# The plan of the expert passes moved from a stage of its own into the mix, and the experts' credits from GpSimd to TensorE

## The reference, cut to what matters

```python
x  = x + mix @ w_out
x  = x + memory_cross_attention(rms_norm(x, g_mem_norm), rms_norm(mem, g_mem_src), ...)
x  = x + moe_ffn(rms_norm(x, g_moe_norm), ...)
# moe_ffn: 32 experts, 4 per token
logits = t @ router_w + router_b
top_logit, top_idx = top_k(logits, 4);  gates = softmax(top_logit)
gu = t[tok] @ w_gate_up[e] + b_gate_up[e]
act = (clip(gu[:, 1::2], -7, 7) + 1) * gate * sigmoid(1.702 * gate)   # gate = min(gu[:, 0::2], 7)
out[tok] += gates * (act @ w_down[e] + b_down[e])
```

## Time and profile before

| | |
|---|---|
| median of 3 runs | 3191.83 us (3190.61 to 3194.59) |
| the profiled execution | 3192.96 us, its span 3190.9 us |
| mean granted TensorE clock | 0.935 |
| PE busy | 2776.5 us, 87% of the span |
| DVE busy | 1158.9 us, 36% |
| ACT busy | 593.1 us, 19% |
| POOL busy | 182.0 us, 6% |
| HBM traffic | 559.44 MB read, 69.88 MB written |

### The profile page before, as it was taken

One profiled execution on the slowest core, in us unless ns is written; L12 is line 12 of the kernel. 1 busy time (PEld: TensorE's weight loads), 2 busy tenths in 40 slices (PEclk: granted clock), 3 DMA queues, 4 the chain that ended last, 5 costly groups with the idle time before them and its releaser, 6 DMA issues.

```text
span 3190.9 us, 41664 instructions
## 1 busy us (share of the span) xinstructions
PE 2776.5 (87%) x12040; PEld 1389.1 (44%) x12041; DVE 1158.9 (36%) x2949; ACT 593.1 (19%) x1582; POOL 182.0 (6%) x188
## 2 busy tenths in 40 slices
PE   6998599999789964999999899999999999999991
PEld 3554466666455631344444334333343443343340
DVE  2776267766446631222221222222212122222125
ACT  1222155555323310010000000100000010000010
POOL 0000000000001010100000100000101000000100
PEclk9999599999899956999999999999999999999995
DMA  8222553030201007766555966677876766646746
GB/s 300 69 65 72 124 156 89 16 75 15 94 34 40 34 14 291 272 230 250 193 188 185 339 241 227 226 291 270 324 272 255 264 222 226 251 172 228 294 182 270
DMA packets 295909, 586.97 MB, mean 184 GB/s; under 512 B 79006, under 2 KB 117918, under 8 KB 274312
## 3 DMA queue, kind: packets, MB, share of 16 engines
q1 hardware_dynamic: 255805, 542.87, 48.1%
q0 software_dynamic: 21152, 38.50, 3.6%
q10 hardware_dynamic: 18859, 4.42, 0.6%
HBM read 559.44 MB, written 69.88 MB: 197 GB/s over the span
## 4 chain that ended last, share of the span: by engine, by line
PE 51%; issue 3%; DMA 3%; DVE 3%; ACT 1%; ACTq 0%; DVEq 0%; POOL 0%; POOLq 0%; SPq 0%
PE ps L1820 30%; PE ps L1904 17%; PE ps L1916 2%; PE ps L1793 2%; DVE x L1778 1%; DMA d_ys<-ys_e,dst 1%; DVE gu L1715 1%; DMA xg<-d_h,src 1%; ACT aT L1629 1%; PE ps L1798 1%; DMA wg<-in_w_gate_up 1%; ACT xT_e L1609 0%; DVE gg L1718 0%; DVEq L1509 0%; DMA src<-d_tok 0%
## 5 line engine op out<-in xcount | busy, mean ns | idle before, releaser
L1820 PE MATMUL ps<-wg,xT_e 128*64 128x512 f32 (+2 forms) x4032 | 1034.3, 598 | 33.8 <-issue 30.4
L1820 PEld LDWEIGHTS ps<-wg,xT_e 128*64 128x64 f32 (+2 forms) x4032 | 398.6, 147 | 639.3 <-issue 634.6
L1904 PE MATMUL ps<-w_rows,aT 128*128 128x512 f32 x1152 | 527.9, 614 | 40.9 <-issue 23.9
L1715 DVE TENSOR_TENSOR gu<-ps,bias 64x512 f32<-64x512 f32 (+2 forms) x252 | 173.6, 689 | 654.8 <-PE ps L1820 632.6
L1904 PEld LDWEIGHTS ps<-w_rows,aT 128*128 128x128 f32 x1152 | 220.4, 196 | 309.6 <-issue 285.6
L1651 ACT ACTIVATE ss<-gg 128x256 f32<-128x256 f32 x146 | 60.8, 416 | 1289.5 <-DVE gg L1718 747.8
L1759 DVE COPY ys_e<-ps 128x1024 f32<-128x1024 f32 x36 | 44.1, 1225 | 622.3 <-PE ps L1904 622.3
L442 PE MATMUL ps<-w_in,hT_a 128*128 128x430 f32 x512 | 194.6, 533 | 6.3 <-DVE hT_a L345 6.3
L793 PE MATMUL ps<-ident_t,sc 128*128 128x128 f32 x880 | 152.1, 290 | 28.2 <-ACT sc L859 24.7
L859 ACT ACTIVATE sc<-sc,nm 128x640 f32<-128x640 f32 (+15 forms) x256 | 161.5, 633 | 53.1 <-DVE nm L901 53.1
L1793 PE MATMUL ps<-ident_e,xg 128*128 128x128 f32 x392 | 72.4, 323 | 101.5 <-DMA xg<-d_h,src 48.4
(11 more groups left out here) (293 smaller groups left out, 2489.3 us busy)
## 6 DMA issues: line engine op xcount, KB each, us to landing
wg<-in_w_gate_up SPq DMA_DIRECT2D x128, 2048.0 KB, 8.1
w_rows<-in_w_down SPq DMA_DIRECT2D x128, 1024.0 KB, 7.9
bias<-in_b_gate_up SPq DMA_DIRECT2D x32, 1024.0 KB, 9.7
wg<-d_ys SPq DMA_DIRECT2D x8, 2048.0 KB, 12.4
d_bias<-d_rev SPq DMA_DIRECT2D x1, 10368.0 KB, 37.9
w_in<-in_w_in SPq DMA_DIRECT2D x1, 6880.0 KB, 23.9
x_a<-in_x POOLq DMA_DIRECT2D x8, 512.0 KB, 3.7
kn<-d_kn SPq DMA_DIRECT2D x8, 512.0 KB
```

What stands on the lines that cost most here:

```text
L1715: read = dve.tensor_tensor(gu[part, :], ps[part, BANK[k][j], :], bias[part, cols], ALU.add)
L1820: mm = pe.matmul(ps[g * kind:(g + 1) * kind, BANK[k][j], :], xT[:, kk, t0:t0 + kind], wg[:, j * groups + g, kk, :], start=(kk == 0), stop= ...
L1904: mm = pe.matmul(ps[:, 2 + 2 * b + h, :], aT[:, j, b * P:(b + 1) * P], wd[:, c, j % 2, h * 512:(h + 1) * 512], start=(j == 0), stop=(j == ...
```

## The change

The plan's constants, tiles and 28 steps move into stage_mix. The steps are a function `plan_passes`, which DVE calls in the last turn straight after the last tile's slot numbers, ahead of the last add into x3. SP loads two more constants in its list (the mix already has the third, iota), and at the end of its stream stores and reloads the plan row. stage_plan is gone with its block and its clearing. In stage_experts the credits are given by PE instead of POOL, ahead of everything else that PE does. No other line is changed.

```diff
@@ stage_mix
+        pidx, allone = sb("pidx", [P, 1]), sb("allone", [P, NE])
+        over_k, npas, ends, done, eq = (sb(n, [P, NE]) for n in ("over_k", "npas", "ends", "donep", "eq"))
+        r, plan = sb("r", [P, 12]), sb("plan_f", [P, 8], I32)
+        steps, over = sb("steps", [P, 4, 7]), sb("over", [P, 3, 7])
...
-                                          "msk rk gmT slot bd x3 ssy ss1 qn ss2").split()}
+                                          "msk rk gmT slot bd x3 ssy ss1 qn ss2 plan").split()}
+        s_plan = sem("x_plan_moved")
         C = CREDIT
-        N_FIRST, N_REST = 5, 9
+        N_FIRST, N_REST = 5, 11
...
                                  (ebase[:, :], e.c_ebase.partition_broadcast(P)),
+                                 (pidx[:, :], e.c_pidx), (steps[:, :, :], e.c_steps.partition_broadcast(P)),
                                  (tok[:, :, :, :], e.c_tok.rearrange("(t p) k o -> p t k o", p=P))):
...
+                sp.wait_ge(m["plan"], C + 1)
+                sp.dma_start(e.d_plan.rearrange("(p n) -> p n", n=8), plan[:, :]).then_inc(s_plan, 16)
+                sp.wait_ge(s_plan, C + 16)
+                sp.dma_start(e.plan[:, :], e.d_plan.rearrange("(o n) -> o n", o=1)).then_inc(s_plan, 16)
+                sp.wait_ge(s_plan, C + 32)
                 for i in range(2):
                     sp.wait_ge(s_h3st[i], C + 16 * (NT // 2))
...
+                def plan_passes():
+                    step(dve.memset(allone[:, :], 1.0))
...
+                    dve.tensor_copy(plan[:, :], r[:, 4:12]).then_inc(m["plan"], 1)
...
                         dve.tensor_copy(slot[:, d, :], slf[:, d, :]).then_inc(m["slot"], 1)
+                    if d == NT - 1:
+                        plan_passes()
@@ stage_plan
-            def _(pool):
-                give_credit(pool, e.sems)
-            def _(sp):
-                sp.dma_start(iota[:, :], e.c_iota.partition_broadcast(P)).then_inc(s_in, 16)
-                sp.dma_start(pidx[:, :], e.c_pidx).then_inc(s_in, 16)
-                sp.dma_start(steps[:, :, :], e.c_steps.partition_broadcast(P)).then_inc(s_in, 16)
-                sp.wait_ge(s_dv, CREDIT + 28)
-                sp.dma_start(e.d_plan.rearrange("(p n) -> p n", n=8), plan[:, :]).then_inc(s_out, 16)
-                sp.wait_ge(s_out, CREDIT + 16)
-                sp.dma_start(e.plan[:, :], e.d_plan.rearrange("(o n) -> o n", o=1)).then_inc(s_out, 16)
-                sp.wait_ge(s_out, CREDIT + 32)
...
@@ stage_experts
             def _(pool):
-                give_credit(pool, e.sems)
...
             def _(pe):
+                give_credit(pe, e.sems)
+
@@ program
         stage_mix(nc, e)
-        stage_plan(nc, e)
         stage_experts(nc, e)
```

More of the change, by code:

```diff
@@ L1203, in normed_y @@
                     dve.tensor_tensor(halves(y[:, k % 2, :]), halves(y[:, k % 2, :]), bcast(sy[:, k, :].unsqueeze(2), [P, 2, 512]), ALU.mult).then_inc(m["yn"], 1)
+                def plan_passes():
+                    step(dve.memset(allone[:, :], 1.0))
+                    step(dve.memset(r[:, :], 0.0))
+                    step(dve.tensor_scalar(npas[:, :], e.cnt[:, :], 0.0, None, ALU.is_gt))
+                    for k in range(1, CAP // PASS):
+                        step(dve.tensor_scalar(over_k[:, :], e.cnt[:, :], float(k * PASS), None, ALU.is_gt))
+                        step(dve.tensor_tensor(npas[:, :], npas[:, :], over_k[:, :], ALU.add))
+                    step(dve.tensor_tensor_scan(ends[:, :], allone[:, :], npas[:, :], 0.0, ALU.mult, ALU.add))
+                    step(dve.tensor_scalar(done[:, :], ends[:, :], pidx[:, 0:1], None, ALU.is_le))
+                    step(dve.tensor_reduce(r[:, 0:1], done[:, :], AX.X, ALU.add))
+                    step(dve.tensor_tensor(over_k[:, :], done[:, :], npas[:, :], ALU.mult))
+                    step(dve.tensor_reduce(r[:, 1:2], over_k[:, :], AX.X, ALU.add))
+                    step(dve.tensor_tensor(r[:, 2:3], pidx[:, :], r[:, 1:2], ALU.subtract))
+                    step(dve.tensor_scalar(r[:, 2:3], r[:, 2:3], float(PASS), None, ALU.mult))
+                    step(dve.tensor_scalar(eq[:, :], iota[:, :], r[:, 0:1], None, ALU.is_equal))
+                    step(dve.tensor_tensor(over_k[:, :], eq[:, :], e.cnt[:, :], ALU.mult))
+                    step(dve.tensor_reduce(r[:, 3:4], over_k[:, :], AX.X, ALU.add))
+                    step(dve.tensor_tensor(r[:, 6:7], r[:, 3:4], r[:, 2:3], ALU.subtract))
+                    step(dve.tensor_scalar(r[:, 6:7], r[:, 6:7], 0.0, None, ALU.max))
+                    step(dve.tensor_scalar(r[:, 4:5], r[:, 0:1], float(NE - 1), None, ALU.min))
+                    step(dve.scalar_tensor_tensor(r[:, 5:6], r[:, 4:5], float(CAP), r[:, 2:3], ALU.mult, ALU.add))
+                    step(dve.tensor_scalar(r[:, 5:6], r[:, 5:6], float(NE * CAP - PASS), None, ALU.min))
+                    step(dve.tensor_scalar(over[:, 0, :], steps[:, 0, :], r[:, 6:7], None, ALU.is_lt))
+                    step(dve.tensor_tensor(steps[:, 1:4, :], steps[:, 1:4, :], bcast(over[:, 0:1, :], [P, 3, 7]), ALU.mult))
+                    step(dve.tensor_reduce(r[:, 7:10], steps[:, 1:4, :], AX.X, ALU.add))
+                    dve.tensor_copy(plan[:, :], r[:, 4:12]).then_inc(m["plan"], 1)
@@ L1401, in _ @@
                         turn(h2[:, :], 2).then_inc(m["h2T"], 1)
[L1405 to L1417, removed]
-            def _(pool):
-                give_credit(pool, e.sems)
-            @block.sync
-            def _(sp):
-                sp.dma_start(iota[:, :], e.c_iota.partition_broadcast(P)).then_inc(s_in, 16)
-                sp.dma_start(pidx[:, :], e.c_pidx).then_inc(s_in, 16)
-                sp.dma_start(steps[:, :, :], e.c_steps.partition_broadcast(P)).then_inc(s_in, 16)
-                sp.wait_ge(s_dv, CREDIT + 28)
-                sp.dma_start(e.d_plan.rearrange("(p n) -> p n", n=8), plan[:, :]).then_inc(s_out, 16)
-                sp.wait_ge(s_out, CREDIT + 16)
-                sp.dma_start(e.plan[:, :], e.d_plan.rearrange("(o n) -> o n", o=1)).then_inc(s_out, 16)
-                sp.wait_ge(s_out, CREDIT + 32)
[L1432 to L1457, removed]
-                step(dve.tensor_reduce(r[:, 3:4], a[:, :], AX.X, ALU.add))
-                step(dve.tensor_tensor(r[:, 6:7], r[:, 3:4], r[:, 2:3], ALU.subtract))
-                step(dve.tensor_scalar(r[:, 6:7], r[:, 6:7], 0.0, None, ALU.max))
-                step(dve.tensor_scalar(r[:, 4:5], r[:, 0:1], float(NE - 1), None, ALU.min))
-                step(dve.scalar_tensor_tensor(r[:, 5:6], r[:, 4:5], float(CAP), r[:, 2:3], ALU.mult, ALU.add))
-                step(dve.tensor_scalar(r[:, 5:6], r[:, 5:6], float(NE * CAP - PASS), None, ALU.min))
-                step(dve.tensor_scalar(over[:, 0, :], steps[:, 0, :], r[:, 6:7], None, ALU.is_lt))
-                step(dve.tensor_tensor(steps[:, 1:4, :], steps[:, 1:4, :], bcast(over[:, 0:1, :], [P, 3, 7]), ALU.mult))
-                step(dve.tensor_reduce(r[:, 7:10], steps[:, 1:4, :], AX.X, ALU.add))
-                step(dve.tensor_copy(plan[:, :], r[:, 4:12]))
```

## The result

The changed kernel takes **3174.69 us** (median of 6 runs, 3171.01 to 3178.0); the kernel before took 3190.6 us on the same chip (6 runs, 3185.11 to 3194.59). The ratio is 0.9945, 95% interval 0.9933 to 0.9957: 15.9 us less. The forecast was 3175. The profiled execution took 3177.3 us with a span of 3175.6, so 15.7 us less than the one of before, where the sum had 16.7.

A forecast was written before the change was run, and what follows sets the result against it. TensorE's expert passes fill most of the span, but the untouched target was the handover through the plan stage, all on the path. 14.16 - 0.3 - 0.16 + 3.0 = 16.7 us off 3192.96 gives 3176.3; median 1.1 lower, 3175 (3171 to 3181).

The forecast's parts named there:

- the sum: Whole kernel: the gains and losses add to 14.16 - 0.3 - 0.16 + 3.0 = 16.7 us saved.
- Step 1: Between mix and experts: removing the plan stage, with its loads, trips and exit, gains 14.16 us.
- step 2: End of the mix: the plan hides beside the last scatters and POOL's drain, with 1.0 us of cover, costing nothing.
- Step 3: Last four scatters of the mix: the plan's DVE steps beside them slow them by 0.3 us, 1.2 at most.
- Step 4: Mix's head: two more POOL credits cost 0.16 us; SP's two extra load issues, about 0.9 us, cost the path nothing.
- Step 5: Experts' start: PE gives credits at 0.15 us each, so the first weight load starts at 3.0 us instead of 2.67.
- Step 6: Experts' start: row-number load goes ahead of weights, first gather 3.4 us earlier; at most 3.1 survives, 3.0 taken.
- The order flipped: Rival at the experts' start: the two loads keep their order, the 3.0 us are missing, 3178.1 us; chance 26%.
- The cover held: Rival at the mix's exit: too thin a cover, from slow DMA trips (3178.3) or POOL locked out (3179.5); 10% together.
- The time given back by the clock: Rival at the experts' start: TensorE stays at 1.2 GHz for 20 us more, losing 10 us; chance 3%.
- The rival on the slower side: Rival in the expert passes: shifted code brings a 2.69 us stall into each of 32 passes, 86 us, 3261; 2%.

The follow-up runs named there:

- after_again: The changed kernel, unaltered, timed again on another chip: 3172.83 us, ratio 0.9937.
- p1_after: The changed kernel, unaltered, timed a third time on another chip: 3175.04 us, ratio 0.9948.
- e2: The kernel before, with only the experts' credits moved from POOL to PE; the plan keeps its stage: 3191.1 us, ratio 0.9987.
- e5: The changed kernel with 28 idle VectorE steps of the plan's own form put before the plan: 3180.83 us, ratio 0.9966.
- e3: The changed kernel, with PE giving the two credits SP's weight loads wait for right after the identity's: 3177.62 us, ratio 0.9943.
- e6: The changed kernel with row numbers loaded as ACT's first instruction and the first gather waiting only for POOL's own clear: 3177.0 us, ratio 0.9953.
- e1: The changed kernel with the experts' credits back on POOL, so only the plan is moved: 3180.69 us, ratio 0.9949.
- p2_plan_only: e1 run again beside the changed kernel on one chip (plan moved, POOL gives the credits): 3177.9 us, ratio 0.9958.
- e4: e1 with SP's first weight load held until ACT has issued its row-number load: 3180.06 us, ratio 0.9949.
- e7: The changed kernel with SP instead of POOL waiting for the scatters to land: 3176.51 us, ratio 0.995.
- e8: The changed kernel with the edits of e6 and e7 together: 3180.3 us, ratio 0.9956.
- p3_sp_waits: e7 run again beside the changed kernel on one chip (SP waits for the scatters): 3177.89 us, ratio 0.9959.

## Why the prediction was right, point by point

**Step 1, the stage removed (14.16), step 2, the plan hidden.** Right. The handover lost 13.76 us in this profile, 13.1 and 14.3 in the other two; the forecast's first two steps less the 0.3 of the third make 13.86. The cover was 0.7 us here, 0.5 in after_again, 0.9 in p1_after, forecast 1.0. What ate at it is the plan's store: I had steps' end to SP's drain at 3.1 us, and it was 3.7 (1191.32 to 1195.0), with 2.10 for the store alone (from 1191.35 to the reload at 1193.46). In after_again it took 3.0, and in the same profile the scatters landed later too, so that POOL's drain ended 11.1 us behind the slots. In the profiles without a plan store beside the scatters (before, e2, e5) it ended 10.1 to 10.3 behind them, in the eight with one, 9.9 to 11.2. That the store delays the landing, or that something else slows both, is what these numbers suggest; neither was tried, and with the shortest store (1.40 us) the drain ended at 9.9, no later than without one.

**Step 3, slower scatters (0.3).** The size was wrong: it is nothing. Beside the plan's steps the scatters took 0.95 to 0.97 us in every profile. What the steps met was small and on DVE: the same comparison took 0.36 us once and 0.18 otherwise, the whole plan 6.15 instead of 5.91. The rate was taken from one form of operation and carried over to others. In the kernel before, 32 scatters lie beside all kinds of DVE work, and only the six that meet the 128x1024 scaling of h_x took over 1.0 us (1.02 to 1.15); the others, beside reductions, copies and adds from PSUM or beside nothing, took 0.95 to 0.96. The Trainium skill (SBUF — State Buffer, the "DVE blocks DMA" trap) has GpSimd locked out of descriptor writing while VectorE runs an operation in a 2-port performance mode, a condition that the prediction left out. Nothing of a lock is seen beside the plan's steps, and no row shows which of them run in such a mode. In this profile 0.4 us did appear, but as a later landing: the drain ended 10.49 us behind the slots, 10.11 before.

**Step 4, the mix's head (0.16).** Right for the credits. POOL gives 61, and ACT's first square starts 4.96 us behind the mix's first load, 4.81 before. SP's two loads more put its next load 18.96 us behind the mix's first (868.91 - 849.95) instead of 18.29 (868.67 - 850.38), 0.7 us later. Whether that costs the path nothing, as forecast, isn't shown: ACT waits for this kind of load in both kernels, and the mix's length scatters by more.

**Step 5, credits at 0.15 us each.** Right: (1205.1 - 1196.9)/54 = 0.152 us. The first weight load starts at 1199.93 - 1196.79 = 3.14 us, forecast 3.0.

**Step 6, the flip (3.0).** Right up to the landing of the weights, and wrong behind it. The trigger was right to the tenth: the row numbers landed in 1.90 us (1.75 forecast), the gather came 3.33 us earlier (3.4), and the last chunk of pass two 3.13 us earlier (3.1). e3 shows that the order of the loads does it for the gather, e6 that the stream caps it.

What failed is the last sentence, "After that pass TensorE is the chain again, and a shift stays a shift". Of the 3.1 us only 0.7 were left at the end of the second pass's gate-up matmuls, since TensorE started them at its low clock, as the stretches above show. In that same pass's down matmuls it was the other way round: before, the clock stood at 0.61 from 1303.92 to 1311.92 and the first 16 took 9.37 us; now it was high and they took 7.13, which put the changed kernel 3.0 us ahead again. The lead keeps changing. Where the same 128 matmuls start in both kernels, it is 3.0 us at 197 us into the stage (1405.72 and 1390.56), -0.1 at 1196 us (2404.66 and 2392.59) and 3.3 at 1807 us (3016.22 and 3000.76). At the end it is 3.2, near the 3.0 forecast. That agreement is luck. From the experts' first instruction to the end of the span, the nine profiles in which the row numbers go first and TensorE gives the credits took 1972.9 to 1982.4 us, mean 1977.0; the four in which they don't (before, e1, p2_plan_only, e3) took 1972.2 to 1982.0, mean 1977.9, and e4 1981.9. One pair of profiles can't show 3 us in that.

The forecast also took the split for granted. With the flip the chunk lands at 65.5 to 66.0 us in eight profiles and at 67.1 in one (p1_after), mean 65.9. Without it, it lands at 66.9, 67.2 and 66.4 us (e1, p2_plan_only, e3), mean 66.8. The flip therefore accounts for about 1 us of the 3.1 there, and the rest was already gone in e1, which still has the old order. The granted clock shows where. These are e1 and the changed kernel from 30 us into the stage (busy PE, PEld, DVE, ACT, POOL, then PEclk, DMA share, GB/s):

```profile
1224.13:1228.13 4.00, 3.96 (x12) 1.69 (x13) 0.00 (x0) 0.00 (x0) 0.84 (x1) 0.63 1.02 418
1228.13:1232.13 4.00, 4.00 (x22) 1.82 (x20) 0.27 (x1) 0.00 (x0) 1.14 (x2) 1.00 1.00 414
```

```profile
1226.79:1230.79 4.00, 4.00 (x22) 1.47 (x20) 0.00 (x0) 0.00 (x0) 0.42 (x1) 1.00 1.02 426
```

In the changed kernel the clock is at its high level of 2.4 GHz by 30 us, in e1 it rises in the four us after that, and before it was at 0.50 there and rose only in the four us after those (0.69 from 1242.92 to 1246.92). So before, TensorE went through more of its first pass at the low level, released the buffers later, and the queues idled. Over all profiles the granted clock from 30 to 34 us was 0.76 to 1.00 in the nine with the flip by TensorE's credits and 0.50 to 0.67 in the other five: earlier rows go with an earlier rise. But e1 rose earlier than before with a gather only 0.3 us earlier, and why is open. The forecast worked with one idle time, 3.4 us, and it had no term for the clock, neither for what it gives in the first pass nor for what it takes in the second.

The timings leave the term open. For it speaks the pair that differs in the credits alone and was run most often: e2 took 3.7 us less than before, with an interval of 1.3 to 7.0 us, so some gain is there. The changed kernel gained 15.9, 21.7 and 17.6 us in three timings, the plan alone 14.1 and 14.7. Against it, e3, which has the old order of the loads, gained 17.2, and the variants that keep the flip and were expected to be as fast or faster (e6, e7, e8 and e7's repeat) gained 17.6, 18.0, 14.3 and 14.7. That the same kernel's gain spans 5.8 us from chip to chip is the reason why no single pair settles a term of 3 us.

**The sum and the rest.** 16.7 forecast, 15.7 in the profile. The missing us isn't in any step: from the mix's first load to the last slots the changed kernel took 335.28 us and the kernel before 333.23, but 333.68 and 333.79 in the changed kernel's other two profiles. e2, whose mix is that of the kernel before, took 330.78, so this stretch scatters by over 2 us without any edit. In 860 to 870 us, TensorE had a granted clock of 0.59 where before it had 0.68, over the same 8.61 us of busy time. The clock moves whole runs: of the six timed runs, the one with a mean granted clock of 0.941 took 3171.01 us, the one with 0.937 took 3177.3. The range, 3171 to 3181, holds that. That the median, 3174.69 us, lies 0.3 from the 3175 forecast is luck: the same kernel's three gains lie 5.8 us apart, and the profile's agreement rests in part on a lead in the experts that comes and goes.

**The rivals.** The order flipped in every profile with the credits on TensorE as the change has them, with a lead of 0.25 to 0.46 us where 0.3 was forecast. The cover held, without much to spare. The time given back by the clock came in a form that the prediction didn't have: no longer stay at the low level at the start, but a fall to it ahead of the second pass, for 2.4 us instead of 10. The rival on the slower side falls: in the later full passes of the chain 128 matmuls take 20.91 to 20.98 us, before and after.

The stall of 2.69 us isn't there any more. In its place the first expert matmul waits longer: 6.63 us of "issue" instead of 4.84, so that it starts only 1.2 us earlier in the stage (24.95 instead of 26.17) though the transposes end 3.0 earlier. In that wait TensorE's sequencer loads plan words and branches, and one branch, past a piece that this pass does not have, is long:

```profile
L1806 PEldq COMPARE_BRANCH  x33: 70/207/1930, 1218.8 to 3049.7; - x33
```

The 1,930 ns are those of 1218.8; before (L1832 there) the same branch took at most 213 ns. All ten profiles with TensorE's credits have one such branch in the first pass, of 0.95 to 3.11 us, and no stall behind it; the four with POOL's have none, and a stall of 2.44 to 2.69 us behind the first matmuls instead. The edit moves TensorE's code by its 55 credits, so the place of the code is a candidate for both. That would fit the Trainium skill (Runtime: NRT & Kernel Launch, "Instruction fetch mechanics"), by which a taken branch whose target isn't in the store waits for a fetch; no row shows the fetch itself.

## What to carry to other kernels

A stage in which only one engine does small dependent steps is worth its whole length on the path, exit and clearing included, once its steps find a place beside a wait that another engine needs anyway; count the cover to a tenth (here 0.4 to 0.9 us), for one more trip through DRAM, 1.4 us at the least, would have used it up. When an edit shifts an issue by some tenths of a us, look for the load from the other queue that stands next to it: which of the two goes first moved the gather by ten times the shift. But follow such a gain to the end of the stage before you count it. A gain upstream of a saturated stream ends at the stream (two us more on the gather brought nothing), and an engine that gets done sooner waits longer, so that TensorE can start its next piece at the low clock.

## What was not expected of the hardware

- A load of row numbers issued up to 0.12 us behind the first 2 MB weight load of another queue landed after 4.97 to 5.24 us (before, e1, p2_plan_only, e3); 0.25 us or more ahead of it, after 1.86 to 1.97 us (the changed kernel, after_again, e2, e5, e6, p3_sp_waits, e8).
- POOL's drain behind indirect DMAs takes 2664 ns to the digit in every profile where POOL has first waited for them; where it hasn't, it ends 3.8 to 4.1 us behind the last scatter, that is sooner than wait and drain together (4.9 to 6.2).
- TensorE gives credits at 0.152 us each, GpSimd at 0.078 ((854.6 - 849.9)/60).
- A kernel that reaches the second pass sooner can start it at half the clock: 23.40 us for 128 matmuls that took 20.98 before.
- When TensorE's granted clock rises in the first pass of the experts differs by some us between kernels that feed it nearly alike, and runs of one kernel differ by 6 us at mean clocks 0.004 apart.
